# GpSimd takes over the multiply by the norm weights at the entries of two squared-ReLU layers

## The reference

```python
def rms_norm(x, g):
    xf = x.astype(jnp.float32)
    y = xf * lax.rsqrt(jnp.mean(xf * xf, axis=-1, keepdims=True) + NORM_EPS)
    return (y * g.astype(jnp.float32)).astype(x.dtype)

def squared_relu_mlp(x, w_up, w_down):
    h = jax.nn.relu(x @ w_up)
    return (h * h) @ w_down

# first_block, DEPTH = 2: mixer 0 is attention, mixer 1 is pooling
    for i in range(DEPTH):
        xn = rms_norm(x, norm_mix[i])
        ...
        x = x + y
        x = x + squared_relu_mlp(rms_norm(x, norm_mlp[i]), mlp_w_up[i], mlp_w_down[i])
    return rms_norm(x, norm_final)
```

## Time and profile before

| | before |
|---|---|
| three runs, us | 1193.29, 1194.12, 1196.0 |
| the profiled execution, us | 1193.4 |
| its span, first to last instruction, us | 1191.6 |
| PE busy | 1132.8 us, 95% of the span |
| DVE busy | 677.9 us, 57% |
| ACT busy | 531.0 us, 45% |
| POOL busy | 41.9 us, 4% |
| mean granted TensorE clock | 0.984 of full speed |

### The profile page before, as it was taken

One profiled execution on the slowest core, in us unless ns is written; L12 is line 12 of the kernel. 1 busy time (PEld: TensorE's weight loads), 2 busy tenths in 40 slices (PEclk: granted clock), 3 DMA queues, 4 the chain that ended last, 5 costly groups with the idle time before them and its releaser, 6 DMA issues.

```text
span 1191.6 us, 17784 instructions
## 1 busy us (share of the span) xinstructions
PE 1132.8 (95%) x7114; PEld 1008.9 (85%) x7114; DVE 677.9 (57%) x936; ACT 531.0 (45%) x644; POOL 41.9 (4%) x69
## 2 busy tenths in 40 slices
PE   4999999999999999997899999999999989999997
PEld 3887799999889999976767999999798768999996
DVE  4745644544664454466635655554765767555554
ACT  4446443443444344345434544334543664443342
POOL 0000000000000000000000000000410310000000
PEclk9999999999999999998979999999999998999999
DMA  9752446556534655544512466556754242556550
GB/s 351 254 179 69 143 157 210 166 187 202 186 104 156 206 170 187 189 128 159 177 36 71 141 188 198 177 176 224 223 177 156 86 134 72 188 177 199 176 176 35
DMA packets 127450, 196.36 MB, mean 165 GB/s; under 512 B 7393, under 2 KB 97633, under 8 KB 127281
## 3 DMA queue, kind: packets, MB, share of 16 engines
q1 hardware_dynamic: 124256, 186.29, 47.5%
q0 software_dynamic: 3152, 9.51, 2.7%
HBM read 194.73 MB, written 1.05 MB: 164 GB/s over the span
## 4 chain that ended last, share of the span: by engine, by line
PE 84%; DVE 9%; ACT 4%; issue 1%; DMA 1%; DVEq 0%; SPq 0%; ACTq 0%
PE ps L1395 26%; PE ps L1397 26%; PE ps L1396 26%; DVE wlo L895 2%; ACT whi L596 1%; DVE xs L1001 1%; ACT junk L627 1%; DMA raw<-attn_w_qkv_in 1%; PE ps L1501 1%; PE ps L1787 1%; PE ps L1785 1%; DVE act_lo L1015 1%; PE ps L1417 1%; DVE x L1046 1%; DVE xs L1042 1%
## 5 line engine op out<-in xcount | busy, mean ns | idle before, releaser
L895 DVE TENSOR_TENSOR wlo<-raw,whi 128x2048 fp32r<-128x2048 f32 (+2 forms) x173 | 389.1, 2266 | 178.9 <-ACT whi L596 177.8
L1395 PE MATMUL ps<-act_hi,whi 128*128 128x256 f32 x1384 | 392.7, 284 | 6.4 <-DVE act_lo L1015 3.4
L1396 PE MATMUL ps<-act_lo,whi 128*128 128x256 f32 x1384 | 391.7, 283 | 0.0
L1397 PE MATMUL ps<-act_hi,wlo 128*128 128x256 f32 x1384 | 391.6, 283 | 0.0
L596 ACT ACTIVATE whi<-raw 128x2048 fp32r<-128x2048 f32 (+2 forms) x172 | 321.2, 1888 | 114.1 <-PE ps L1397 99.4
L1395 PEld LDWEIGHTS ps<-act_hi,whi 128*128 128x128 f32 x1384 | 263.5, 190 | 11.3 <-issue 8.3
L1396 PEld LDWEIGHTS ps<-act_lo,whi 128*128 128x128 f32 x1384 | 263.6, 190 | 2.0
L1397 PEld LDWEIGHTS ps<-act_hi,wlo 128*128 128x128 f32 x1384 | 263.6, 190 | 0.0
L1397 PE MATMUL ps<-whi,hlo 128*128 128x512 f32 x400 | 156.8, 392 | 0.0
L1396 PE MATMUL ps<-wlo,hhi 128*128 128x512 f32 x400 | 156.8, 392 | 0.0
L1395 PE MATMUL ps<-whi,hhi 128*128 128x512 f32 x400 | 156.2, 390 | 0.0
(11 more groups left out here) (157 smaller groups left out, 889.8 us busy)
## 6 DMA issues: line engine op xcount, KB each, us to landing
raw<-mlp_w_up_in SPq DMA_DIRECT2D x32, 1024.0 KB, 6.4
raw<-mlp_w_down_in SPq DMA_DIRECT2D x32, 1024.0 KB, 4.9
raw<-ffn_w_gate_in SPq DMA_DIRECT2D x22, 1024.0 KB, 5.3
raw<-ffn_w_up_in SPq DMA_DIRECT2D x22, 1024.0 KB, 5.4
raw<-ffn_w_down_in SPq DMA_DIRECT2D x22, 1024.0 KB, 4.8
raw<-attn_w_qkv_in SPq DMA_DIRECT2D x12, 1024.0 KB, 8.6
raw<-w_kv_shared_in SPq DMA_DIRECT2D x8, 1024.0 KB, 7.0
raw<-attn_w_o_in SPq DMA_DIRECT2D x4, 1024.0 KB, 4.9
```

The costliest lines, as they stand in the source:

```text
L895: nc.vector.tensor_tensor(wlo[:, s, 0:width], raw[:, s, 0:width], whi[:, s, 0:width].bitcast(F32), ALU.subtract).then_inc(lo_ready, 1)
L1395: nc.tensor.matmul(dst, lhsT=left[0], rhs=right[0], start=start, stop=False, **kw)
L1396: nc.tensor.matmul(dst, lhsT=left[0], rhs=right[1], start=False, stop=False, **kw)
L1397: return nc.tensor.matmul(dst, lhsT=left[1], rhs=right[0], start=False, stop=stop, **kw)
```

## The change

At the entries "mlp0" and "mlp1" the four multiplications by the norm weights go from VectorE to GpSimd. VectorE issues only the sums (and at "mlp1" the scaling), and then goes on to the `act_lo` splits. GpSimd waits for each quarter of `x`, multiplies, and after the fourth releases the row itself. Its list of row loads is cut at two places, so that the multiplications stand between loads. Nothing changes at the other entries ("mix0", "pre0", "fpre0", "kvsrc", "pre1", "fpre1"), where `gained` stays on VectorE.

```diff
-            for name in ROWS[1:ROW["pre1"] + 1]:
+            def gained_here(name):
+
+                wait_row(pool, name)
+                for p in range(4):
+                    h, t, cols = quarter(name, p)
+                    pool.wait_ge(x_ready, 4 * XR[name] + p + 1)
+                    nc.gpsimd.tensor_tensor(xs[:, t, cols], x[:, t, cols], row(name)[:, cols], ALU.mult)\
+                        .then_inc(xs_ready, 1)
+                pool.wait_ge(xs_ready, 4 * XSR[name] + 4)
+                pool.sem_inc(row_used, 1)
+
+            for name in ("mlp0", "mix1", "pool_scale"):
+                load_row(name)
+            gained_here("mlp0")
+            for name in ("mlp1", "final"):
+                load_row(name)
+            gained_here("mlp1")
+            for name in ROWS[ROW["pre0"]:ROW["pre1"] + 1]:
                 load_row(name)
...
+            HERE_NOT = ("mlp0", "mlp1")
...
-                    if then:
+                    if then and then not in HERE_NOT:
                         gained(then, p)
...
                 link(nc.vector.tensor_tensor(xs[:, t, cols], bank(2 * t + h), row("pool_scale")[:, cols], ALU.mult))
                 nc.vector.tensor_tensor(x[:, t, cols], x[:, t, cols], xs[:, t, cols], ALU.add).then_inc(x_ready, 1)
-                gained("mlp1", p)
             release_row()
```

## The result

| | before | after |
|---|---|---|
| executions, us | 20: 1193.05 to 1196.37 | 20: 1185.48 to 1194.72 |
| median, us | 1195.61 | 1186.4 |
| ratio of the times | | 0.9947, interval 0.993 to 0.9963 |
| the profiled execution, us | 1193.4 | 1194.24 |
| its mean granted clock | 0.984 | 0.982 |

The account below looks back on a forecast made before the run. TensorE, busy 95% of the span, was taken as the bound. Entry terms +0.03 and -0.92 gave -0.9 us: 1193.4 becomes 1192.5, forecast as 1193.2 for the median; range 1192.4 to 1194.0, over the cases 1190.9 to 1195.8.

Parts of the forecast that it names:

- The bound and the carrying: TensorE, busy 95% of the span, bounds the kernel; the first squared-ReLU layer carries an entry's gain or loss one for one.
- The bracket: Profile put the second "up" chunk of "mlp1" down to a late `wlo`; read as misleading, same 0.78 us idle in "mlp0".
- D: Time GpSimd needs for one multiply at either entry: taken as 1.3 us, low end 0.97, far end 3.13.
- Entry "mlp0": First entry: GpSimd's fourth multiply ends at 137.56, 0.74 us later than VectorE's; first product at 138.44, a loss of 0.03 us.
- M: TensorE's first product of the layer at each entry: forecast 138.44 at "mlp0" and 346.01 at "mlp1", 0.82 us behind T.
- T: Moment TensorE starts to transpose the last quarter at each entry: forecast 137.62 at "mlp0" and 345.19 at "mlp1".
- Entry "mlp1": Second entry: `x` comes each 1.83 us, first product at 346.01 in place of 346.93, a gain of 0.92 us.
- the meeting: At "mlp1", VectorE's operation reading two SBUF tiles is held up by GpSimd's multiply: 0.5 us taken, bounds 0 and 0.73.
- full-lock rival: At "mlp1" each VectorE operation waits for GpSimd's instruction to end: quarter 2.06 us, in all 0.2 us gain, 1193.9; chance 0.17.
- The sum: Both entries together: +0.03 - 0.92 = -0.9 us, or 5 x D - 7.4, nothing at D = 1.48.
- The clock: Rival: clock 1.00 in both windows, but longer gaps at "mlp0" could lower it, each us of products costing up to one more.
- the slow case: Rival: GpSimd's multiplies slow at both entries, a loss from 1.48 us each, 1194.8 to 1206.5; with low clock, chance 0.13.

Follow-up runs that it names:

- the kernel with "mlp1" alone: GpSimd multiplies at entry "mlp1" only, "mlp0" as before; against the kernel before: ratio 0.9978, five executions at 1186.32 to 1187.24, seven at 1193.12 to 1195.49 us.
- the kernels with three fills: Kernels after and before with filler products in three TensorE waits (5.6, 1.5, 1.5 us); medians 1183.71 and 1184.72 us, ratios 0.9914 and 0.9918 against the kernel before.

## Why the prediction was wrong

**The bound and the carrying** were right. TensorE carried each entry's gain one for one: 0.35 us at the second "up" chunk of "mlp0", 0.97 at that of "mlp1". The bracket was read rightly too: the second "up" chunk again waits 0.78, now put down to the relu in both layers.

**D.** Taken 1.3, measured 1.27. The Trainium skill (GPSIMD Engine Reference, "Performance versus the Vector engine") led by a quarter of its figure to an estimate of 1.12 us; the trace, at 1.27, is above that.

**Entry "mlp0"** was mis-sized: a loss of 0.03, measured a gain of 0.45. The four multiplies ended 4.95 us behind their start, at 137.16, where I had 4 x 1.3 + 3 x 0.08 = 5.44. M came 0.75 behind T, not 0.82. The mechanism stood: GpSimd was the last, and TensorE started 0.05 behind it.

**Entry "mlp1"**: forecast T 345.19 and M 346.01, measured 345.09 and 345.83. Of M's 1.10, 0.35 to 0.45 is inherited from "mlp0"; the kernel with "mlp1" alone wins 0.62 by its trace, against my 0.92. The step that was off is the meeting: VectorE's operation lost 0.64, 0.58 and 0.57 us rather than 0.5. In mechanism that is nearer to the full-lock rival, which I had at 0.17: a quarter took 339.97 - 338.08 = 1.89 us, between my 1.83 and that rival's 2.06. The Trainium skill (SBUF — State Buffer, "Who interferes with whom") calls the pair of ports that the two engines share an exclusive lock; this trace agrees, since each L1278 that met a multiply ended 0.55 to 0.56 behind it (339.89 against 339.34), most of its own 0.69.

**The sum** for the entries, -0.9 us, came out: -1.03 in the profiled execution, about -1.0 between the kernels whose clock holds. In part that was luck: "mlp0" gave some 0.4 more than I had, "mlp1" 0.3 less.

**The step that failed** is the one that made a sum of entries into a time: "The clock. It is 1.00 in both windows ... Longer gaps at "mlp0" could bring the lower level ... I count it with the slow case." I asked about the clock only where the edit is, and only as a loss. Everything behind was taken as carried unchanged, a term put at nothing without a row for it. But the second block held some 34 us at half clock, between 558 and 992, and 24 of them stood behind waits of 5.6 and 1.5 us. The same waits do not always bring the same stretches: in the eight traces it goes by where the waits fall, counted from the start of the full clock. Shifted by -1.0 us, 22 of 32 executions end 7 to 8 us earlier, and the one of them seen in a trace keeps the full clock through the attention at 596; unshifted, none of 85 is that fast. Of the 6.4 us between the means about 1.0 is the entries', and 5.4 the clock's. The forecast had no rival of this kind on either side. What it wrote down as "Wrong altogether: a granted clock below 1.00 behind either entry" pointed the right way and would still have looked at the wrong place.

What speaks for this cause: the gain vanishes when the shift is taken back with GpSimd's work left in (1.0004), it appears without GpSimd when the work is shifted later by 1.8 us (0.9958), and with the waits filled both kernels have it and their traces differ by the 1.0 us of the entries. The rule of the Trainium skill that bears on it (TensorE: Matmul & The Clock Gate, "Part 1: The HAM clock gate") is that the gate watches TensorE's activity on a clock of its own that does not start with the kernel, so that executions of one kernel differ; the two levels of one kernel here agree, and so does the start of the long full-clock stretch at 22.4 to 25.5 us.

**What stays open.** Which level a given execution takes can't be told ahead: in the eight traces it goes with the position of the wait behind the start of the full clock, but no run tested that, and the executions without a trace show only their mean clock. Why filling the first wait alone left the kernel after on three levels (1186, 1190, 1192.6) and the kernel before below 1187.1 was not settled, nor what parts the two groups, 1 to 2 us apart, of the kernels with three fills.

## What to carry to other kernels

Before an edit is priced, find every stretch of the whole trace with a granted clock below 1.00 and the wait ahead of it: a shift of 1 us upstream can move such a stretch in or out, which here was worth some seven times the edit's own 1 us in an execution, and 5.4 us in the mean. Weigh a stretch by what TensorE does in it: 13.7 us at half clock cost 6.2 in the attention, where TensorE is busy throughout, and filling away the late ones of 3.4 and 6.8 gave 0.0 and 0.2. Repeat a kernel until both its levels have been seen, and compare kernels with the waits filled if the edit's own worth is asked. Better than luck with the shift is to remove the cause: three groups of filler products in TensorE's waits won 9.8 us on the kernel before (the means, 1184.98 to 1194.8; ratio 0.9918), more than the change did (0.9947).

## What the runs showed of the hardware

- Two waits of 1.47 us, at 586.18 and 593.50, stood before 13.7 us at half clock; with both filled and nothing else changed the stretch was gone in the trace, and six of six executions lay at 1187.0 to 1188.9, where none of 85 without the fillers is below 1192.87.
- At half clock a product of 128x256 took 690 ns by its record against 438; 13.7 us at half clock cost the attention 6.2 us.
- GpSimd's multiply of two 128x512 float32 inputs took 1.26 to 1.27 us, started 1.23 apart where several stood in a row, and a VectorE operation with two SBUF inputs that met it ended 0.55 to 0.56 behind it and took 1.26 to 1.33 in place of 0.69. A VectorE operation with one input in PSUM kept its 0.68 beside it. GpSimd's 128x256 operation with one input had delayed VectorE by only 0.19.
- Its first multiply cost no more than the others: four in 4.95 us, including the first.
